# Start of the recurrence stage: earlier page copies, reordered loads and later scores of chunk 0

## What is computed

```python
z = h @ lp['w_in']
o_g, s_gla = gla_scan(gq * d**-0.5, gk, gv, log_a, gla_s0)        # 4 heads x 64, chunked
k_cmp = rmsnorm(compress_rows(rows_full[:, :, 0], ...))            # over the paged cache rows of each request
v_cmp = compress_rows(rows_full[:, :, 1], ...)
x = x + mix @ w_out
x = x + (relu(rmsnorm(x) @ w_up) ** 2) @ w_down

# gla_scan, one chunk
bcum = cumsum(log_a)                                               # decays within the chunk
scores = einsum('bhtd,bhsd,bhtsd->bhts', q, k, exp(bcum_t - bcum_s))   # causal pairs
o = scores @ v + (q * exp(bcum)) @ S
S = exp(b_end) * S + (k * exp(b_end - bcum))^T v
# compress_rows: blocks of 32 rows with stride 16, hid = rows @ w1 (+ bias), silu, @ w2
```

## Time and profile before

| | us |
|---|---|
| runs | 1842.54, 1835.23, 1833.45 |
| median | 1835.23 |
| profiled execution, its own time | 1845.73 |
| span of the profile | 1843.9 |
| recurrence stage | about 666.7 to 869.3 of the span |

### The profile page before, as it was taken

The page is one execution under the profiler, slowest core; times in us unless marked ns, Lnnn a source line. Parts: engine busy times, 40 slices in busy tenths (PEclk is TensorE's granted clock), DMA queues, the critical chain, the costliest instruction groups (busy, mean ns, idle before and its releaser), DMA issues. The chain is left out here.

```text
span 1843.9 us, 32359 instructions
## 1 busy us (share of the span) xinstructions
PE 1736.9 (94%) x12908; PEld 1612.6 (87%) x12908; DVE 1050.9 (57%) x1867; ACT 633.7 (34%) x1142; POOL 170.1 (9%) x203
## 2 busy tenths in 40 slices
PE   6999999979999979999946999999999999999998
PEld 6989999968888868887624999999999999999998
DVE  6363584238877746666766675444444444444445
ACT  6523332137655544444443454111111111111111
POOL 1000000012222242223012000000000000000000
PEclk7989999969999989999867999999999999999999
DMA  6641265360000146764875651111111111111102
GB/s 184 118 100 35 58 161 149 115 172 24 14 2 1 47 137 234 243 234 162 192 192 167 180 159 55 47 46 45 45 45 45 45 45 45 45 45 45 45 24 92
DMA packets 180898, 177.18 MB, mean 96 GB/s; under 512 B 51564, under 2 KB 163268, under 8 KB 177140
## 3 DMA queue, kind: packets, MB, share of 16 engines
q1 hardware_dynamic: 173924, 132.92, 25.7%
q0 software_dynamic: 2304, 33.56, 4.8%
q10 hardware_dynamic: 4560, 9.18, 1.8%
HBM read 139.60 MB, written 40.23 MB: 98 GB/s over the span
## 5 line engine op out<-in xcount | busy, mean ns | idle before, releaser
L59 PE MATMUL pm<-hH,wuH 128*128 128x344 f32 x768 | 246.3, 321 | 0.0
L61 PE MATMUL pm<-hH,wuL 128*128 128x344 f32 x768 | 245.0, 319 | 0.0
L60 PE MATMUL pm<-hL,wuH 128*128 128x344 f32 x768 | 245.0, 319 | 0.0
L59 PE MATMUL pm<-hidH,weights 128*128 128x344 f32 x720 | 230.7, 320 | 0.0
L60 PE MATMUL pm<-hidL,weights 128*128 128x344 f32 x720 | 230.3, 320 | 0.0
L61 PE MATMUL pm<-hidH,weights 128*128 128x344 f32 x720 | 230.0, 319 | 0.0
L59 PE MATMUL pz<-hH,winH 128*128 128x344 f32 x600 | 200.1, 334 | 1.6 <-DVE hL L845 1.6
L60 PE MATMUL pz<-hL,winH 128*128 128x344 f32 x600 | 193.9, 323 | 0.0
L61 PE MATMUL pz<-hH,winL 128*128 128x344 f32 x600 | 193.9, 323 | 0.0
L3328 DVE SCALAR_TENSOR_TENSOR act<-pm,onat 128x344 f32<-128x344 f32 x96 | 49.3, 516 | 239.8 <-PE pm L61 239.4
L3339 DVE TENSOR_TENSOR onat<-pm,onat 128x344 f32<-128x344 f32 x256 | 129.0, 514 | 68.9 <-PE pm L61 68.9
(11 more groups left out here) (613 smaller groups left out, 3473.4 us busy)
## 6 DMA issues: line engine op xcount, KB each, us to landing
uact<-in_w_up_dram SPq DMA_DIRECT2D x15, 1024.0 KB, 6.9
hs<-in_w_down_dram SPq DMA_DIRECT2D x15, 1024.0 KB
raw<-in_w_in_dram SPq DMA_DIRECT2D x24, 512.0 KB, 3.7
hold<-vS_scratch SPq DMA_DIRECT2D x8, 1024.0 KB, 14.4
wo<-in_w_out_dram SPq DMA_DIRECT2D x12, 512.0 KB
act<-in_w_out_dram SPq DMA_DIRECT2D x12, 512.0 KB, 5.2
zT_scratch<-zb ACTq DMA_DIRECT2D x8, 516.0 KB, 2.6
hold<-in_x_prompt_dram SPq DMA_DIRECT2D x8, 512.0 KB, 4.2
```

The lines of the kernel that those rows point to most:

```text
L59: nc.tensor.matmul(out, wH, mH, start=start and k == 0, stop=False)
L60: nc.tensor.matmul(out, wH, mL, start=False, stop=False)
L61: last = nc.tensor.matmul(out, wL, mH, start=False, stop=stop and k == n - 1)
```

## The change

SyncE issues `load_w1(0)` ahead of `load_z(0)`. GpSimd issues `gather(0, 1)` after the five memsets instead of before them, and `keys(0)` after the first group of masks. ScalarE runs `copy_fill(0, 0)` before `sizes(0)` and `copy_fill(0, 2)` between `sizes(0)` and `decays(0)`. TensorE gets three matmuls of 128x512 in slot 1 of iteration 0, whose result nobody reads. Chunk 0's levels move: level 0 to slot 8, level 1 to slot 10, levels 2 and 3 to slot 11, levels 4 and 5 to slot 0 and levels 6 and 7 to slot 1 of iteration 1; the merges move with them. The other chunks keep their slots.

```diff
-        first_level = lambda c: 6 if c < NCH - 1 else 4
+        LATE = {8: (0,), 10: (1,), 11: (2, 3)}
+        LATER = ({0: (4, 5), 1: (6, 7)}, {0: (6,), 1: (7,)})
+        def levels_at(it, n):
+            if it == 0:
+                return LATE.get(n, ())
+            first = 6 if it < NCH - 1 else 4
+            return (n - first,) if first <= n < first + 8 else ()
+        def levels_over(it, n):
+            return LATER[min(it - 1, 1)].get(n, ()) if it else ()
 # SyncE
+                load_w1(0)
                 load_z(0)
-                load_w1(0)
                 load_z(1)
 # GpSimd
                 nc.gpsimd.memset(qbd[:, :, :], 0.0).then_inc(q_zeroed, 1)
-                gather(0, 1)
 ...
                 nc.gpsimd.memset(lvl[:, :, :].bitcast(I32), 1).then_inc(zeroed, 1)
-                keys(0)
+                gather(0, 1)
                 pool.wait_ge(zeroed, 1)
 ...
                 last.then_inc(masked, 1)
+                keys(0)
                 pool.wait_ge(masked, 1)
 # TensorE, in slot n of iteration it
-                        if n < 2 and it:
-                            level(it - 1, n + 6)
-                        if first_level(it) <= n < first_level(it) + 8:
-                            level(it, n - first_level(it))
+                        if it == 0 and n == 1:
+                            for _ in range(3):
+                                nc.tensor.matmul(og[:, :], ident[:, :], vnat[:, 0, :], start=True, stop=True)
+                        for l in levels_over(it, n):
+                            level(it - 1, l)
+                        for l in levels_at(it, n):
+                            level(it, l)
 # ScalarE
+                copy_fill(0, 0)
                 sizes(0)
+                copy_fill(0, 2)
                 decays(0)
 ...
-                        if n in by_act and it < NCH:
+                        if n in by_act and it < NCH and (it, n) not in ((0, 0), (0, 2)):
                             copy_fill(it, n)
 # VectorE: merge(...) in the same slots as level(...)
-                        if n < 2 and it:
-                            merge(it - 1, n + 6)
+                        for l in levels_over(it, n):
+                            merge(it - 1, l)
 ...
-                        if first_level(it) <= n < first_level(it) + 8:
-                            merge(it, n - first_level(it))
+                        for l in levels_at(it, n):
+                            merge(it, l)
```

## The result

The changed kernel is slower, by 0.3%: median 1841.05 us (1835.83 to 1848.37, 20 runs) against 1836.45 (1830.31 to 1844.09, 20 runs), ratio 1.0029, 95% interval 1.0017 to 1.0041. That is 5 us in 1836. The forecast was +3 us and "no change" by the 0.5% bound.

A forecast was written before the change was run, and what follows sets the result against it. TensorE bounds the kernel, with 8.7 us wasted at the recurrence stage's start. Gather landing 697.9 plus 7.85 puts `fill(1, 2)` at 705.75 against 702.73: +3.0, median 1835.2 to 1838, range 1830 to 1845.

The forecast's parts named there:

- the likeliest case: Start of chunk 0: gather packets delay `load_z(0)`, `keys(0)` starts at 678.6, weights held up too; +3 to +4 us, chance 0.50.
- the prediction's own sign: Listed test: the prediction is wrong if the shift at `fill(1, 2)` is not that at the stage's end.
- ScalarE, TensorE's front: Chunk 0's start: moved copies delay factors 0.6 us; added matmuls cost nothing, clock full at 671.5, `fill(0, 6)` reached at 678.8.
- Doubled levels: Two levels in one slot leave merges uncovered: 1.1, 1.1 and 2.0 us idle; `fill(1, 0)` to `fill(1, 2)` 7.85 instead of 3.71.
- Loads: late z: Chunk 0's loads: gather packets get over `load_z(0)`, `keys(0)` starts at 678.6, next gather lands at 697.9; +3.0 us.
- issued at 669.2 they start at 671 to 673.5: Second gather in chunk 0: its packets start within 2 us if undisturbed, but by 4.3 us behind its issue as before.
- Second gather: Chunk 0: issued 1.8 us later, it lands between 677.7 and 681.8, taken as 681; TensorE waits 2.2 us, clock fall up to 1.7.
- `fill(1, 0)` set by the next gather: Start of iteration 1: TensorE, ready at 693.9, waits 1 us or more for the gather landing at 694.6 or 697.9.
- early z: Rival at chunk 0's loads: z lands before gather packets, `keys(0)` starts at 675.3, next gather lands at 694.6; -0.3 us, chance 0.25.
- GpSimd: Chunk 0's masks: first group free; second and third, 5.3 us before, take 0 to 1.6 us more beside `queries(0)`, taken as 0.8.
- the shift reaches the end whole: After `fill(1, 2)`: old order, TensorE busy without a gap, so the +3.0 us shift there carries unchanged to the stage's end.
- rival (c): Chunk 0 into iteration 1: gaps keep TensorE's clock at half from 672.6 past `fill(1, 2)`; +11 us, 1846, chance 0.08.

The follow-up runs named there:

- e5: The changed kernel profiled once more with nothing altered; median 1838.54 us (one run).
- e1: The kernel before with only the change's placement of chunk 0's levels and merges; median 1844.43 us, ratio 1.0035 to before.
- e9: The kernel before with only chunk 0's level 6 moved into slot 1 of iteration 1, ahead of level 7; median 1847.51 us (one run).
- e10: The kernel before with only chunk 0's level 4 moved from slot 10 into slot 11, ahead of level 5; median 1840.57 us (one run).
- e2: The changed kernel with chunk 0's levels back in their old slots; median 1835.31 us, ratio 0.9987 to before.
- e12: The same kernel as e2, measured again to narrow the interval; median 1836.35 us, ratio 0.9981 to before.
- e8: e2 with `load_z(1)` and `load_w1(1)` held until the second gather landed, first half's store before them, `keys(0)` after the second mask group; ratio 1.0004 to before.
- e4: The changed kernel with `gather(0, 1)` issued ahead of the memsets again; median 1847.90 us, ratio 1.0059 to before.
- e6: The changed kernel without the three added matmuls; median 1842.76 us, ratio 1.0037 to before.
- e7: The changed kernel with `load_z(0)` ahead of `load_w1(0)` again; median 1841.03 us, ratio 1.0023 to before.
- e3: The changed kernel with one level per slot: 0 to 4 in slots 7 to 11, 5 to 7 in iteration 1's slots 0 to 2; ratio 1.0015 to before.

## Why the prediction was right, and where it was not

The time was right: +3 forecast, +5 measured, inside 1830 to 1845. The sum was made for slot 2 of iteration 1, and there it holds: +3.0 forecast, 39.0 - 36.0 = +3.0 in the first profiles, 39.1 - 35.4 = +3.7 in the second. But that it came out to the tenth there is luck: `keys(0)` started 3.7 us earlier than the likeliest case had it (8.2 after the start, forecast 11.9), and four terms that were too small took the same 3.7 back: from `keys(0)` to the next gather's issue +1.7, that gather +1.3, TensorE itself not ready at its landing +0.3, the pairs +0.4 (the gather's length is that of e5, where its landing is shown). And one price is missing behind slot 2. By the prediction's own sign, that the shift at slot 2 be that at the stage's end, it is wrong in this step: +3.0 and +8.5 in the first profiles, 4.3 of that being the late gather, and +3.7 and +5.3 in the second.

*ScalarE, TensorE's front.* Right. The copies ran at 662.1 and 664.6, the clock was full until 673.7, and `fill(0, 6)` was due at 11.8 us after the start, forecast 12.1.

*Doubled levels.* Right, and shown by e1, e9 and e10: 1.0, 0.9 and 2.0 us against 1.1, 1.1 and 2.0, and 8.3 against 7.85 to slot 2. It is the term that decides the sign: with it the change is +5, without it (e2, e12) -1 to -3 by the medians.

*Loads: late z.* Wrong. The step that failed is "issued at 669.2 they start at 671 to 673.5", from which followed that the gather's packets start over `load_z(0)` and hold it up. That is 4.3 to 6.8 us after the start; they came at 7.1, and z had landed at 6.8. And the other half of the step, that z starves once they flow, did not hold either: in e8 they came at 5.1, and z landed at 6.8 all the same.

The prediction gave a reason for the early packets: the rule of the Trainium skill's page "SBUF — State Buffer", section "SBUF: two separate sides", that GpSimd can't write a DMA's descriptors while VectorE runs an operation in a 2-port mode. It was carried further than that rule goes, since VectorE's differences are TENSOR_TENSOR operations with two inputs. And it did not decide here: the differences ended 3.0 us after the start, VectorE's copies 4.4, and with the same VectorE timeline the packets came at 7.1 in the changed kernel and at 5.1 in e8.

*Second gather.* Its landing was forecast 14.3 us after the start and was 15.7; TensorE waited 3.9 instead of 2.2. The wait brought the clock down, which the prediction had allowed for with up to 1.7 us: TensorE was busy 5.57 us at half clock, so it cost about 2.8 (an estimate, half of 5.57).

*`fill(1, 0)` set by the next gather.* Half right. That gather was issued at 20.6 after the start (forecast 19.3 and 22.5). In e5, where its landing is shown, it took 9.9 us instead of 8.6 and landed at 30.5. The prediction had read the median of the earlier trace rows, 8.9, as the longest of the others; in the kernel before they took up to 11.0. TensorE took it up at 30.75 (e5 30.9), without a wait, where 1 us or more was forecast: it had itself been held by the second gather, by the half clock behind it and by the pair (2, 3). The masks held nobody: they were ready at 679.6, before merge 0 (681.7) had its level. "Late z" had 31.2, "early z" 27.9. So z was early, and the number is nearly that of late z: the likeliest case got its time by the mechanism of another. In e1, e4, e6 and e7 the same gather did hold TensorE, for 0.9, 0.4, 0.3 and 0.8 us.

*GpSimd.* The masks took 7.7 us after `keys(0)`, not 5.3 plus 0 to 1.6: the second group of seven selects took 4.7 beside VectorE's multiply and differences, 2.2 before. Of the first group, which ran when VectorE was idle, the 128x128 select took 0.28, against 2.11 in the earlier trace rows.

*Behind slot 2.* The step "the shift reaches the end whole" left out the clock. Of the seven profiles with the pair (6, 7) it fell in chunk 1 in six (changed, e4, e5, e6, e7, e9; not in e1), and in none of the seven others. In the changed kernel chunk 1 grew by 5.7 us, of which 4.55 stand before slot 2, so the rest is 1.2; in e9 it is 1.2 as well (3.7 less 2.5), in e5 1.5. That is the part between the +3 at slot 2 and the measured +5. The prediction had a fall of the clock in the wait for the gather and, as rival (c), over the whole of chunk 0, but none behind the pairs; it was a short one (3.4 us), in the place where the waits are.

## What to carry to other kernels

Before work is moved out of a crowded stretch, price the place it moves to: here 1 to 3 us were gained at the start, and 4.6 paid in two slots of the next iteration and 1.2 to 1.5 behind them, because two users of one PSUM tensor in one slot have nothing between them to hide the merge, and one of them stood behind an unrelated chain of the other engine. A wait of TensorE costs more than its length when it brings the clock down (e9: 2.0 us of waiting, 3.7 of time). And the indirect gather here, which shares the DMA engines with a loaded queue, was moved forward by issuing less ahead of it (e8); an earlier place in GpSimd's program alone did not do it (e4).

## What had not been expected of the hardware

- The second gather's landing did not follow its issue (it took 15.0 us when issued 1.5 us earlier than in the changed kernel, 13.5 there, and 10.4 with two loads held back), and GpSimd's issue itself took 3.31, 1.81 and 1.06 us in different surroundings.
- A fall of the clock for 3.4 us behind a single wait of 2.0 us (e9), and behind waits of 1.0, 0.9 and 2.0 in five profiles of six (not in e1), while single waits of 1.0 (e10) and 1.1 (e3) brought none there.
- VectorE's copy of the queries, 64x32, took 2.53 us beside GpSimd's memsets in e4, against 0.21.
- The same code ahead of the stage takes 659.2 to 666.7 us, and the rest behind it 967.3 to 975.0, so single spans of this kernel can't carry a difference under 8 us.
